# Recurrence levels of a chunked scan on one TensorE: 64 query columns in place of 128 in the products and the masked copies

## The chip, the cores and the metric

The kernel runs on one core of one Trainium2 chip. The metric is the device time of one execution in microseconds (us); the time before is the median of three runs. TensorE is called PE, VectorE DVE, ScalarE ACT, GpSimd POOL and SyncE SP, as in the profile.

## What is computed

The reference is a two-layer hybrid block (convolution, attention, a gated recurrence, a Fourier mix) followed by a second block (latent attention, a state-space model, a feed-forward network), on 1024 positions and 256 positions of context, all in float32. The change lies in the gated recurrence of the first block. Its reference, cut to the core:

```python
def step(state, inp):
    qc, kc, vc, lf = inp
    a = jnp.cumsum(lf, axis=2)
    a_last = a[:, :, -1:, :]
    s_new = jnp.exp(a_last)[:, :, 0, :, None] * state + jnp.einsum(
        "bhsk,bhsv->bhkv", kc * jnp.exp(a_last - a), vc)
    ...
    inter = jnp.einsum("bhtk,bhkv->bhtv", qc * jnp.exp(a), state)
    diff = a[:, :, :, None, :] - a[:, :, None, :, :]
    dec = jnp.exp(jnp.where(causal, diff, -jnp.inf))
    scores = jnp.einsum("bhtk,bhsk,bhtsk->bhts", qc, kc, dec)
    intra = jnp.einsum("bhts,bhsv->bhtv", scores, vc)
    return s_new, inter + intra
```

There are four heads of 64 channels, two directions and two layers, so `recurrence` runs four times.

## The kernel before

**Levels.** The kernel works on chunks of 128 positions. The decay between key s and query t inside a chunk can't be split into a factor of s and a factor of t for all pairs at once, so the pairs are sorted into seven levels, `LEVELS = [64, 32, 16, 8, 4, 2, 1]` (h), and an eighth step for s = t. At level h the chunk falls into blocks of 2h positions; in the forward direction the first half of each block holds keys and the second half queries (`query_half` is 1; in the backward direction it is 0). The tile `x` (`X[j % 2][:, l, c, :]`, 128 positions for each level l and each pair of heads c) holds the scaled keys in the one half and the scaled queries in the other. The function `halves` gives views of both.

**One chunk on each engine** (u counts chunks, j those with an output):
- POOL (L1167, L1168) writes differences of `a` into `x`, 14 operations of 128 elements per chunk, for a chunk two further on, when the products that read this buffer are done.
- ACT exponentiates `eq` (L1180), `ke` (L1184, twice) and all of `x` (L1190, 1792 elements), and copies the turned keys `ket` out of PSUM (L1196).
- PE does, in this order: the products of levels 0 and 1 (L1327), two transposes of `ke` (L1303), the products of levels 2 to 5 (L1327), in layer 0 a piece of another matrix product (the modulation, `mods.products`, L2640 and L2643, weights read from memory), the products of level 6 and of the diagonal (`q,key`), the state products (L1337), and last the eight output products (L1347 and L1348), which need the finished `sc`. One product is four matmuls, one for each head: stationary operand `x` (64 rows, 128 columns), moving operand also `x`. The heads of a pair lie on partitions 0 to 63 and 64 to 127 and write different PSUM banks. A float32 matmul shows as two records.
- DVE gathers the scores: eight `copy_predicated` (L1259) per chunk, which take from PSUM into `sc` those elements that the level's mask selects. Between them it scales the level operands of the next chunk: after the second copy `ke` and `qe` (L1220, L1225), from the third copy on two `tensor_tensor` of 128 elements (L1238) per level. Then come the state update (L1271) and the copy or addition of the output into `o` (L1281, L1283).

**What sets the order.** Everything is written by hand. The eight steps are done in pairs g (two levels, one PSUM region for each parity of g). A copy waits for `products` of its pair; the first matmul of a pair waits until the copies of the pair two before are done (`masked`, two copies per pair): so the last pair (level 6 and diagonal) waits for the copy of level 3. The output products wait for all eight copies. I call the eight copies c0 to c7.

Layer 0 has ten chunks with output per direction and the modulation product in each, layer 1 has eight and no modulation product (its two context chunks give a state only).

Of the kernel before, what the change touches and what calls it, by code (L numbers as in the profile page):

```python
# [9 lines left out]
U32 = mybir.dt.uint32  # L10
F32R = mybir.dt.float32r

P = 128
# [7 lines left out]
HD = 64  # L21
# [986 lines left out]
LEVELS = [64, 32, 16, 8, 4, 2, 1]  # L1008
NL = len(LEVELS)
# [102 lines left out]
def recurrence(k, direction, q, key, a, v, o, outputs, lay, mods=None):  # L1112
# [7 lines left out]
    nc, ps, d = k.nc, k.ps, k.d  # L1120
# [5 lines left out]
    sc = lay("sc", [P, 2, 2, P])  # L1126
# [15 lines left out]
    def halves(view, h):  # L1142

        r = view.rearrange("p c (n s h) -> p c n s h", s=2, h=h)
        return [r[:, :, :, i, :] for i in range(2)]

    with nc.Block() as block:
# [53 lines left out]
        @block.vector  # L1201
        def _(dve):
            n = [0]

            def link(ins):

                ins.then_inc(chain, 1)
                n[0] += 1
                dve.wait_ge(chain, n[0])

            dve.memset(sc[:, :, :, :], 0.0)
            link(dve.memset(S[0][:, :, :], 0.0))
            dve.wait_ge(masks_in, 16)

            def scale(u):

                t = order[u]
                qs, ks = q[:, :, t * P:(t + 1) * P], key[:, :, t * P:(t + 1) * P]
                dve.wait_ge(exped, u + 1)
                dve.tensor_tensor(ke[:, :, :], ke[:, :, :], ks, ALU.mult).then_inc(scaled, 1)  # L1220
                if want[u]:
                    j = n_out[u]
                    if j >= 2:
                        dve.wait_ge(o_ready, j - 1)
                    dve.tensor_tensor(qe[j % 2][:, :, :], eq[u % 2][:, :, :], qs, ALU.mult).then_inc(scaled, 1)  # L1225

            def scale_level(u, l):

                if u >= len(order) or not want[u]:
                    return  # L1230
                t, j, h = order[u], n_out[u], LEVELS[l]
                qs, ks = q[:, :, t * P:(t + 1) * P], key[:, :, t * P:(t + 1) * P]
                if l == 0:
                    dve.wait_ge(x_exped, j + 1)
                xh = halves(X[j % 2][:, l, :, :], h)
                f = [halves(ks, h)[0], halves(qs, h)[1]] if query_half else [halves(qs, h)[0], halves(ks, h)[1]]
                for i in range(2):
                    ins = dve.tensor_tensor(xh[i], xh[i], f[i], ALU.mult)  # L1238
                if l == NL - 1:
                    ins.then_inc(scaled, 1)  # L1240

            def finish(u):

                t = order[u]
                if not want[u] and u + 1 < len(order):
                    scale(u + 1)
                    for l in range(NL):
                        scale_level(u + 1, l)
                if want[u]:
                    j = n_out[u]  # L1250
                    if j >= 1:
                        dve.wait_ge(o_ready, j)
                    for l in range(NL + 1):
                        g, half = PAIRS * j + l // 2, l % 2
                        dve.wait_ge(products, g + 1)
                        if l:
                            dve.wait_ge(masked, (NL + 1) * j + l)
                        b = 2 * (g % 2)
                        dve.copy_predicated(  # L1259
                            sc[:, :, :, :].rearrange("p a b c -> p (a b) c"),  # L1260
                            masks[:, l, :].bitcast(U32).unsqueeze(1).to_broadcast([P, 4, P]),
                            ps[:, b:b + 2, half * 256:half * 256 + 256].rearrange("p a (b c) -> p a b c", b=2)
                        ).then_inc(masked, 1)
                        if l == 1 and u + 1 < len(order):
                            scale(u + 1)
                        if l >= 2:
                            scale_level(u + 1, l - 2)
                    scale_level(u + 1, NL - 1)
                dve.wait_ge(s_ready, u + 1)
                for c in range(2):  # L1270
                    ins = dve.scalar_tensor_tensor(S[(u + 1) % 2][:, c, :], S[u % 2][:, c, :],  # L1271
                                                   eq[u % 2][:, c, edge:edge + 1],
                                                   ps[:, 4, BR + c * HD:BR + (c + 1) * HD], ALU.mult, ALU.add)
                ins.then_inc(state_out, 1)
                if want[u]:
                    j = n_out[u]
                    dve.wait_ge(o_ready, j + 1)
                    src = ps[:, 6:8, 0:P].rearrange("p a (c e) -> p a c e", c=2)
                    dst = o[:, t, :].rearrange("p (c a e) -> p a c e", c=2, a=2)
                    if direction == 0:  # L1280
                        dve.tensor_copy(dst, src).then_inc(o_out, 1)  # L1281
                    else:
                        dve.tensor_tensor(dst, src, dst, ALU.add).then_inc(o_out, 1)  # L1283
                dve.wait_ge(state_out, u + 1)

            scale(0)
            for l in range(NL):
                scale_level(0, l)
            for u in range(len(order)):
                finish(u)  # L1290

        @block.tensor
        def _(pe):
            scales = 0
            for u, t in enumerate(order):
                j = n_out[u]

                def turn_keys():
                    pe.wait_ge(scaled, base + 1)
                    if u >= 1:  # L1300
                        pe.wait_ge(state_out, u)
                    for c in range(2):
                        mm = pe.transpose(ps[:, 4, c * P:(c + 1) * P], ke[:, c, :], k.ident[:, :])  # L1303
                    mm.then_inc(ke_t, 1)

                base = scales
                scales += 1
                if not want[u]:
                    turn_keys()
                else:  # L1310
                    scales += 2
                    pe.wait_ge(scaled, scales)
                    for l in range(NL + 1):
                        g, half = PAIRS * j + l // 2, l % 2
                        if g >= 2 and half == 0:
                            pe.wait_ge(masked, 2 * (g - 1))
                        for h in range(4):
                            c, par = divmod(h, 2)
                            p0 = par * HD
                            if l < NL:  # L1320
                                x = X[j % 2][p0:p0 + HD, l, c, :]
                                y = x
                            else:
                                x = key[p0:p0 + HD, c, t * P:(t + 1) * P]
                                y = q[p0:p0 + HD, c, t * P:(t + 1) * P]
                            o0 = half * 256 + c * P
                            mm = pe.matmul(ps[:, 2 * (g % 2) + par, o0:o0 + P], x, y, start=True, stop=True)  # L1327
                        if half:
                            mm.then_inc(products, 1)
                        if l == 1:  # L1330
                            turn_keys()
                        if l == 5 and mods:
                            mods.products(pe, mods.first + u)
                pe.wait_ge(ket_out, u + 1)
                for h in range(4):
                    c, p0 = h // 2, (h % 2) * HD
                    mm = pe.matmul(ps[p0:p0 + HD, 4, BR + c * HD:BR + (c + 1) * HD], ket[:, h * HD:(h + 1) * HD],  # L1337
                                   v[:, t, h * HD:(h + 1) * HD], start=True, stop=True)
                mm.then_inc(s_ready, 1)
                if want[u]:  # L1340
                    if j >= 1:
                        pe.wait_ge(o_out, j)
                    pe.wait_ge(masked, (NL + 1) * (j + 1))
                    for h in range(4):
                        c, p0 = h // 2, (h % 2) * HD
                        out = ps[:, 6 + h % 2, c * HD:(c + 1) * HD]
                        pe.matmul(out, sc[:, h % 2, c, :], v[:, t, h * HD:(h + 1) * HD], start=True, stop=False)  # L1347
                        mm = pe.matmul(out, qe[j % 2][p0:p0 + HD, c, :], S[u % 2][p0:p0 + HD, c, :], start=False, stop=True)  # L1348
                    mm.then_inc(o_ready, 1)
# [1960 lines left out]
```

## Time and profile before

| | |
|---|---|
| Median of three runs | 5587.69 us (5578.17 to 5592.48) |
| The profiled execution | 5573.2 us, of which the span is 5571.4 us |
| PE busy | 4363.7 us (78% of the span) |
| DVE busy | 2794.4 us (50%) |
| Mean granted PE clock, whole span | 0.861 of full |
| The four recurrences together (from the first operation to the last output) | 617.1 us |

Busy time of an engine is the sum of its instructions' durations; the granted clock is the share of 2.4 GHz that PE was given, and in the rows it is either 0.5 (1.2 GHz, here "the low level") or 1.0 (2.4 GHz, "the high level"). Times in rows count from the start of the span.

### The profile page before, as it was taken

The numbers are of one execution on the slowest core, as the hardware profiler recorded it, in microseconds if no ns is written. First come the engines' busy times: TensorE is split into PE (matmuls) and PEld (weight loads), VectorE is DVE, ScalarE is ACT, GpSimd is POOL, SyncE is SP. The second block draws the span as 40 slices with busy tenths as digits, with TensorE's granted clock in tenths as the row PEclk, the third lists the DMA queues.
The fourth block names the chain that finished last, engine by engine and source line by source line (L and its number), as shares of the span: only waits on it lengthen the run. The fifth ranks groups of instructions, "written<-read, shape, count | busy, mean of one in ns | idle before, by whom it ended". The sixth has DMA issues, their size and how long they took to land. (4 is left out here: it accounts for less than half of the span.)

```text
span 5571.4 us, 56250 instructions
## 1 busy us (share of the span) xinstructions
PE 4363.7 (78%) x21480; PEld 3260.8 (59%) x21480; DVE 2794.4 (50%) x3679; ACT 1861.5 (33%) x3198; POOL 1655.8 (30%) x1452
## 2 busy tenths in 40 slices
PE   5758868678776984747876999998673868899898
PEld 4644557566664563536663565656552656688676
DVE  2354446564535545565543445452446755466556
ACT  3321342323432244232341333332331434344333
POOL 1321132324432132222331121212223635233355
PEclk7968887769987996757988999999886979899999
DMA  4000013223400000000400000002100044211133
GB/s 145 16 19 0 8 60 120 85 74 111 147 16 19 1 16 19 8 4 24 145 30 29 4 7 4 4 1 91 46 1 2 1 170 153 63 46 46 65 129 124
DMA packets 173533, 285.88 MB, mean 51 GB/s; under 512 B 43402, under 2 KB 98698, under 8 KB 173268
## 3 DMA queue, kind: packets, MB, share of 16 engines
q1 hardware_dynamic: 172516, 282.07, 15.0%
q8 instruction: 173, 2.83, 0.2%
q0 software_dynamic: 608, 0.08, 0.1%
q14 instruction: 92, 0.75, 0.0%
q10 hardware_dynamic: 144, 0.15, 0.0%
HBM read 257.01 MB, written 25.26 MB: 51 GB/s over the span
## 5 line engine op out<-in xcount | busy, mean ns | idle before, releaser
L303 POOL TENSOR_TENSOR w_low<-w,w_high 128x512 fp32r<-128x512 f32 (+2 forms) x336 | 505.3, 1506 | 1293.6 <-ACT w_high L294 1293.3
L315 DVE TENSOR_TENSOR x_low<-buf_a,x_high 128x1280 fp32r<-128x1280 f32 (+4 forms) x336 | 369.7, 1101 | 834.1 <-ACT x_high L290 833.7
L332 PE MATMUL ps<-x_high,w_high 128*128 128x256 f32 (+1 forms) x1344 | 499.3, 372 | 93.6 <-POOL w_low L303 86.7
L290 ACT CAST x_high<-buf_a 128x1280 fp32r<-128x1280 f32 (+4 forms) x336 | 310.1, 923 | 777.8 <-PE ps L334 657.6
L945 ACT ACTIVATE pt<-ps 128x512 f32<-128x512 f32 (+1 forms) x488 | 289.6, 594 | 743.9 <-PE ps L888 742.3
L2779 POOL TENSOR_TENSOR w_low<-w,w_high 128x1024 fp32r<-128x1024 f32 x170 | 413.0, 2433 | 347.5 <-ACT w_high L3001 347.4
L898 PE MATMUL ps<-pt,v 128*128 128x512 f32 (+1 forms) x976 | 504.6, 599 | 0.0
L333 PE MATMUL ps<-x_low,w_high 128*128 128x256 f32 (+1 forms) x1344 | 491.2, 365 | 0.0
L334 PE MATMUL ps<-x_high,w_low 128*128 128x256 f32 (+1 forms) x1344 | 486.2, 362 | 0.0
L3031 PE MATMUL ps<-w_high,x_high 128*128 128x512 f32 x896 | 369.3, 412 | 130.3 <-POOL w_low L2779 92.7
L969 DVE TENSOR_REDUCE mx<-ps 128x1 f32<-128x1280 f32 (+1 forms) x200 | 289.7, 1449 | 341.6 <-PE ps L855 340.2
L332 PEld LDWEIGHTS ps<-x_high,w_high 128*128 128x128 f32 x1344 | 263.0, 196 | 172.9 <-issue 70.6
L3032 PE MATMUL ps<-w_low,x_high 128*128 128x512 f32 x896 | 361.0, 403 | 0.0
L3033 PE MATMUL ps<-w_high,x_low 128*128 128x512 f32 x896 | 360.2, 402 | 0.0
L1327 PE MATMUL ps<-x 64*128 64x128 f32 x2016 | 223.0, 374 | 103.0 <-DVE x L1238 87.2
L3001 ACT CAST w_high<-w 128x1024 fp32r<-128x1024 f32 x170 | 178.4, 1049 | 369.8 <-PE ps L3033 369.6
L886 PE MATMUL ps<-q_high,k_high 97*128 97x512 f32 (+3 forms) x488 | 289.7, 594 | 11.1 <-DVE q_low L982 11.1
L332 PE MATMUL ps<-w_high,x_high 128*128 128x512 f32 (+2 forms) x608 | 218.4, 359 | 99.2 <-POOL w_low L303 98.7
L991 DVE RECIPROCAL rec<-ps 64x512 f32<-64x512 f32 (+1 forms) x52 | 168.1, 3232 | 249.5 <-PE ps L898 249.5
L2335 PE MATMUL ps<-x_high,w_high 128*128 128x512 f32 x704 | 278.6, 396 | 13.2 <-DVE x_low L2430 13.2
L3031 PEld LDWEIGHTS ps<-w_high,x_high 128*128 128x128 f32 x896 | 175.5, 196 | 191.3 <-issue 152.8
L334 PEld LDWEIGHTS ps<-x_high,w_low 128*128 128x128 f32 x1344 | 261.7, 195 | 40.5
(388 smaller groups left out, 9354.7 us busy)
## 6 DMA issues: line engine op xcount, KB each, us to landing
w<-in_w_out SPq DMA_DIRECT2D x26, 2048.0 KB, 7.9
w<-in_w_mod SPq DMA_DIRECT2D x24, 2048.0 KB, 8.1
w<-in_w_down SPq DMA_DIRECT2D x15, 2048.0 KB, 7.8
w<-in_w_in SPq DMA_DIRECT2D x12, 2048.0 KB, 10.8
w<-in_w_up SPq DMA_DIRECT2D x22, 1024.0 KB, 6.5
w<-in_w_in SPq DMA_DIRECT2D x16, 1024.0 KB, 5.0
x<-in_x SPq DMA_DIRECT2D x16, 512.0 KB, 3.5
scratch_x<-x SPq DMA_DIRECT2D x16, 512.0 KB, 5.3
```

Source lines behind the costliest of these rows:

```text
L290: act.copy(xh[i % NX][:, 0:s["tn"]], x_of(s)).then_inc(x_high, 1)
L303: pool.tensor_tensor(wl[i % NW][:, 0:n], w_of(s), wh[i % NW][:, 0:n].bitcast(F32), ALU.subtract).then_inc(w_low, 1)
L315: dve.tensor_tensor(xl[i % NX][:, 0:s["tn"]], x_of(s), xh[i % NX][:, 0:s["tn"]].bitcast(F32), ALU.subtract).then_inc(x_low, 1)
L332: pe.matmul(g["out"], lhs[0][:, :], rhs[0][:, :], start=(s["kk"] == 0), stop=False)
L333: pe.matmul(g["out"], lhs[0][:, :], rhs[1][:, :], start=False, stop=False)
L334: mm = pe.matmul(g["out"], lhs[1][:, :], rhs[0][:, :], start=False, stop=s["last"])
L886: pe.matmul(o, hi, qh[u % 2][r0:r1, 0:nq], start=True, stop=False)
L898: pe.matmul(ps[:, 6 + u % 2, 0:w["nq"]], w["v"](i), pt[g % NPT][:, 0:w["nq"]], start=(i == 0), stop=(i == n - 1)).then_inc(pv_done, 1)
L2779: pool.tensor_tensor(wl[i % NW][:, :], ws.tile(s["chunk"])[:, s["kk"] % PER, :], wh[i % NW][:, :].bitcast(F32), ALU.subtract).then_inc(w_l ...
L3031: pe.matmul(o, a[:, t], wh[i % NW][:, c], start=(s["kk"] == 0), stop=False)
L3032: pe.matmul(o, a[:, t], wl[i % NW][:, c], start=False, stop=False)
L3033: mm = pe.matmul(o, b[:, t], wh[i % NW][:, c], start=False, stop=s["last"])
```

## The change

Of the 128 columns of a level's scores the mask selects only those at query positions, which are 64. The change makes the moving operand of each level product the query half alone (64 columns, contiguous for h = 64, and in runs of h with a step of 2h otherwise), puts the two levels of a pair side by side in 256 columns of PSUM for each pair of heads, and copies under the mask only the 64 query columns of each head, into the same places of `sc`. The diagonal step keeps 128 columns in both. The stationary operand stays all 128 columns of `x`. The number and order of instructions and all waits stay.

```diff
-                        dve.copy_predicated(
-                            sc[:, :, :, :].rearrange("p a b c -> p (a b) c"),
-                            masks[:, l, :].bitcast(U32).unsqueeze(1).to_broadcast([P, 4, P]),
-                            ps[:, b:b + 2, half * 256:half * 256 + 256].rearrange("p a (b c) -> p a b c", b=2)
-                        ).then_inc(masked, 1)
+                        heads = ps[:, b:b + 2, :].rearrange("p a (c x) -> p (a c) x", c=2)
+                        if l < NL:
+                            h = LEVELS[l]
+                            n_blocks = P // (2 * h)
+                            to = sc[:, :, :, :].rearrange("p a c (n s h) -> p (a c) n s h", s=2, h=h)[:, :, :, query_half, :]
+                            which = masks[:, l, :].rearrange("p (n s h) -> p n s h", s=2, h=h)[:, :, query_half, :]
+                            dve.copy_predicated(
+                                to, which.bitcast(U32).unsqueeze(1).to_broadcast([P, 4, n_blocks, h]),
+                                heads[:, :, half * HD:half * HD + HD].rearrange("p g (n h) -> p g n h", h=h)
+                            ).then_inc(masked, 1)
+                        else:
+                            dve.copy_predicated(
+                                sc[:, :, :, :].rearrange("p a c t -> p (a c) t"),
+                                masks[:, l, :].bitcast(U32).unsqueeze(1).to_broadcast([P, 4, P]),
+                                heads[:, :, half * HD:half * HD + P]).then_inc(masked, 1)
...
                                 x = X[j % 2][p0:p0 + HD, l, c, :]
-                                y = x
+                                y = halves(X[j % 2][p0:p0 + HD, l, :, :], LEVELS[l])[query_half][:, c]
...
-                            o0 = half * 256 + c * P
-                            mm = pe.matmul(ps[:, 2 * (g % 2) + par, o0:o0 + P], x, y, start=True, stop=True)
+                            o0, m = c * 256 + half * HD, HD if l < NL else P
+                            mm = pe.matmul(ps[:, 2 * (g % 2) + par, o0:o0 + m], x, y, start=True, stop=True)
```

The first chunk of the first recurrence on PE, as the program issues it before the change. A row gives the line, the output and inputs, the output's partitions x columns, and how many follow each other:

```order
L1327 MATMUL ps<-x_140_5781 128x128 x8
L1303 MATMUL ps<-ident_49,ke_5787 128x128 x2
L1327 MATMUL ps<-x_140_5781 128x128 x16
L2640 MATMUL ps<-w_2_50,act_c_55 2x128 x32
L2643 MATMUL ps<-bias_135_5777,one_56 2x128 x4
L1327 MATMUL ps<-x_140_5781 128x128 x4
L1327 MATMUL ps<-q_4404,key_4406 128x128 x4
```

The same place after the change (line numbers are ten higher):

```order
L1337 MATMUL ps<-x_140_5781 128x64 x8
L1313 MATMUL ps<-ident_49,ke_5787 128x128 x2
L1337 MATMUL ps<-x_140_5781 128x64 x16
L2650 MATMUL ps<-w_2_50,act_c_55 2x128 x32
L2653 MATMUL ps<-bias_135_5777,one_56 2x128 x4
L1337 MATMUL ps<-x_140_5781 128x64 x4
L1337 MATMUL ps<-q_4404,key_4406 128x128 x4
```

Nothing has moved; the 28 level matmuls of a chunk stream 64 columns where they streamed 128.

On DVE, the same chunk from the copy of level 0 on, before the change (the last number is what one instruction writes per partition):

```order
L1259 COPY_PREDICATED sc_5789<-masks_5790,ps 128x512 x2
L1220 TENSOR_TENSOR ke_5787<-ke_5787,key_4406 128x256
L1225 TENSOR_TENSOR qe_145_5786<-eq_143_5784,q_4404 128x256
L1259 COPY_PREDICATED sc_5789<-masks_5790,ps 128x512
L1238 TENSOR_TENSOR x_141_5782<-x_141_5782,key_4406 128x2x64
L1238 TENSOR_TENSOR x_141_5782<-x_141_5782,q_4404 128x2x64
L1259 COPY_PREDICATED sc_5789<-masks_5790,ps 128x512
```

And after it:

```order
L1265 COPY_PREDICATED sc_5789<-masks_5790,ps 128x4x64
L1265 COPY_PREDICATED sc_5789<-masks_5790,ps 128x8x32
L1220 TENSOR_TENSOR ke_5787<-ke_5787,key_4406 128x256
L1225 TENSOR_TENSOR qe_145_5786<-eq_143_5784,q_4404 128x256
L1265 COPY_PREDICATED sc_5789<-masks_5790,ps 128x16x16
L1238 TENSOR_TENSOR x_141_5782<-x_141_5782,key_4406 128x2x64
L1238 TENSOR_TENSOR x_141_5782<-x_141_5782,q_4404 128x2x64
L1265 COPY_PREDICATED sc_5789<-masks_5790,ps 128x32x8
```

Here too only sizes change: seven of the eight copies write 256 elements per partition in place of 512, in shorter runs with each level (the eighth, for the diagonal, keeps 512).

## Rows read from the trace of the kernel before

**Rows 1.** The page, part 1: busy us (share of the span) xinstructions.
```profile
PE 4363.7 (78%) x21480; PEld 3260.8 (59%) x21480; DVE 2794.4 (50%) x3679; ACT 1861.5 (33%) x3198; POOL 1655.8 (30%) x1452
```

**Rows 2.** Windows (length, PE, PEld, DVE, ACT, POOL busy, clock, DMA), layers 0, 1.
```profile
811.00:981.00 170.00, 137.14 (x1620) 115.20 (x1620) 107.78 (x272) 40.31 (x91) 55.66 (x140) 0.70 0.36 122
2184.00:2321.70 137.70, 94.86 (x740) 79.74 (x740) 87.34 (x224) 26.65 (x49) 44.45 (x112) 0.70 0.02 5
```

**Rows 3.** Timeline, one layer 0 chunk: start us, us, engine, line [idle before <-releaser].
```profile
901.60 2.12 PE L1327 MATMUL ps<-x 64*128 64x128 f32 x15
...
903.85 1.56 DVE L1259 COPY_PREDICATED sc<-masks,ps 128x512 f32<-128x512 uint32 x2 [1.49 <-PE ps L1327]
904.26 2.44 PE L1327 MATMUL ps<-x 64*128 64x128 f32 x32
905.67 0.43 DVE L1220 TENSOR_TENSOR ke<-ke,key 128x256 f32<-128x256 f32 x1 [0.26 <-ACT ke L1184]
906.64 1.93 PE L2640 MATMUL ps<-w,act_c 128*2 128x128 f32 x64
907.26 0.29 DVE L1238 TENSOR_TENSOR x<-x,key 128x128 f32<-128x128 f32 x1 [0.17 <-ACT x L1190]
908.50 0.40 PE L2643 MATMUL ps<-bias,one 1*2 1x128 f32 x8
909.37 0.61 PE L1327 MATMUL ps<-q,key 64*128 64x128 f32 x8
910.95 0.71 DVE L1259 COPY_PREDICATED sc<-masks,ps 128x512 f32<-128x512 uint32 x1
```

**Rows 4.** Timeline, c6 of the chunk before that one.
```profile
895.35 0.73 DVE L1259 COPY_PREDICATED sc<-masks,ps 128x512 f32<-128x512 uint32 x1 [0.16 <-PE ps L1327]
```

**Rows 5.** Timeline, one layer 1 chunk, copies c0, c3, c6, c7 and the outputs.
```profile
2462.36 1.56 DVE L1259 COPY_PREDICATED sc<-masks,ps 128x512 f32<-128x512 uint32 x2 [1.49 <-PE ps L1327]
...
2466.18 0.72 DVE L1259 COPY_PREDICATED sc<-masks,ps 128x512 f32<-128x512 uint32 x1
...
2469.45 0.72 DVE L1259 COPY_PREDICATED sc<-masks,ps 128x512 f32<-128x512 uint32 x1
2470.66 0.71 DVE L1259 COPY_PREDICATED sc<-masks,ps 128x512 f32<-128x512 uint32 x1
2471.52 0.41 PE L1347 MATMUL ps<-v,sc 128*128 128x64 f32 x2 [3.02 <-DVE sc L1259]
2476.28 0.42 DVE L1283 TENSOR_TENSOR o<-ps,o 128x256 f32<-128x256 f32 x1 [3.07 <-PE ps L1348]
```

**Rows 6.** Timeline, the output copies that bound the periods.
```profile
839.33 0.42 DVE L1281 COPY o<-ps 128x256 f32<-128x256 f32 x1 [3.25 <-PE ps L1348]
965.10 0.42 DVE L1281 COPY o<-ps 128x256 f32<-128x256 f32 x1 [4.00 <-PE ps L1348]
2214.06 0.42 DVE L1281 COPY o<-ps 128x256 f32<-128x256 f32 x1 [3.27 <-PE ps L1348]
2307.33 0.42 DVE L1281 COPY o<-ps 128x256 f32<-128x256 f32 x1 [3.04 <-PE ps L1348]
2492.37 0.42 DVE L1283 TENSOR_TENSOR o<-ps,o 128x256 f32<-128x256 f32 x1 [3.33 <-PE ps L1348]
```

**Rows 7.** Windows around the chunk of rows 3.
```profile
898.30:905.10 6.80, 6.80 (x38) 5.66 (x40) 2.43 (x7) 0.73 (x3) 2.57 (x7) 0.50 0.48 184
905.10:911.90 6.80, 5.27 (x124) 4.37 (x122) 6.37 (x18) 3.15 (x7) 1.82 (x5) 1.00 0.28 66
```

**Rows 8.** Line L1942: matmuls of 16 columns on 128-column weights; one window of it.
```profile
L1942 PE MATMUL ps<-dta,tri x40: 374/374/392, 4238.5 to 4246.8; 128*128 128x16 f32 x40
...
4239.00:4246.00 7.00, 7.00 (x35) 7.00 (x34) 0.00 (x0) 0.00 (x0) 0.00 (x0) 0.50 0.00 0
```

**Rows 9.** Timeline, eight records of 64 columns and what follows them.
```profile
4318.06 1.00 PE L2128 MATMUL ps<-xd,e 128*128 128x64 f32 x8
4318.87 0.48 PE L2113 MATMUL ps<-sums_at_t,sums_at_s 128*128 128x512 f32 x1
```

## The prediction

> **What bounds the kernel now.** Over the whole span PE is the busiest engine at 78% [rows 1], but this says little about four stages of 617 us together. So I read the windows of the recurrences first: one in layer 0 takes 170 us with PE busy 137 and DVE 108, one in layer 1 137.7 us with 94.9 and 87.3, and the mean granted clock is 0.70, below the 0.861 of the kernel [rows 2]. Neither engine is full: it is a ring of waits, once round per chunk. The ring's period comes from the output copies: (965.10 - 839.33)/8 = 15.72 us in layer 0 and (2307.33 - 2214.06)/6 = 15.55 us in layer 1 [rows 6].
>
> Next the timeline of a chunk, following in the brackets what ended each idle time. In layer 1 [rows 5]: c0 starts at 2462.36; the reader should see that c3 starts 3.82 later, c7 8.30 later, and the output products 9.16 later, released by DVE. From there PE runs the eight output products and the next chunk's first two levels, and only then can the next c0 start: at the low clock level the period is 2492.37 - 2476.28 = 16.09, so this second half takes 16.09 - 9.16 = 6.93. The ring is thus DVE (c0 to c7), PE (outputs, levels 0 and 1), DVE. Two waits inside the DVE half are for ACT, not for a copy: `ke` at 905.67 (idle 0.26) and the first scaling at 907.26 (idle 0.17, until the big exponential is done) [rows 3]. So what c0, c1 and c2 take is hidden behind ACT; from 907.26, just before c3, DVE runs on its own. In layer 0 a third wait can come in: PE has the modulation product (64 records) ahead of level 6 and the diagonal. Those end at 909.37 + 0.61 = 909.98, 0.97 before c6 in this chunk [rows 3], but in the chunk before it c6 waited for PE [rows 4]. There PE and DVE are level.
>
> **The change, part by part.**
>
> *Copies, 512 to 256 elements.* No 256-element masked copy is in the trace. The nearest: a `tensor_tensor` of 256 elements takes 0.43 and one of 128 takes 0.29 [rows 3], 1.1 ns per element; 256 fewer elements save 0.27 or 0.28 of 0.72. The scalings at L1238 have the same broken-up runs and the one at h = 64 is no faster than its fellows, so I charge nothing for the short runs. c0 to c2 lie behind ACT: nothing. c3 to c6 are on the path: 4 x 0.27 = 1.07 us per chunk at most, c7 is unchanged. Bounds: 0 if runs cost what is saved, 1.1.
>
> *Level products, 128 to 64 moving columns.* Here the stationary operand decides. 35 records of 16 columns on weights of 128 columns fill a window of 7.00 us at the low level, 0.20 each [rows 8]. The level products of 128 columns use the two row halves side by side, so their records come in pairs: 15 records in 2.12 us at the low level, with the tail of the last one in it (a record lasts 0.37 in a slot of 0.20 in rows 8): 0.25 per pair or a little less [rows 3]. At the high level eight records of 64 columns take 4318.87 - 4318.06 = 0.81, 0.10 each [rows 9], and 16 pairs of 128 columns, the first of them still at the low level, 906.64 - 904.26 = 2.38, 0.15 per pair [rows 3]. So an eighth of the columns does not bring a record below 0.20; half of them brings nothing. The sum takes 0 per record; bound: half of it, 0.1 per pair at the low level, 0.8 for levels 0 and 1. The Trainium skill, TensorE: Matmul & The Clock Gate, section "Back-to-back issue gap", gives the spacing of an isolated matmul as proportional to its moving columns; by it these products would take half, which is rival 3, and the trace with its 0.20 for 16 columns does not bear it out where each record loads new weights.
>
> *The clock.* This is the term I weigh most. Now the low level lasts through the output products and levels 0 and 1, PE busy all of 6.80 us, and turns high at 905.1, when 128-column products have run since before 901.60 [rows 3, 7]. In rows 8 PE is just as busy, 7.00 of 7.00 us, yet the level stays low to the end: the records there stream 16 columns and spend the rest on weights. So a PE busy with loading weights does not raise the level; one that streams does. After the change each level record streams half of what its slot holds, as the output products do, under which the level doesn't rise either. I take it that in layer 1 the level now stays low all through, and in layer 0 it rises only under the modulation product, whose moving side is unchanged.
>
> The same page of the Trainium skill, in its part on the HAM clock gate, says that how busy PE has recently been decides the clock. Read as the profile's busy share it would leave the level as it is, which is rival 1; rows 8 (busy 7.00 of 7.00, clock 0.50) speak against that reading.
>
> **Layer 1 with the low level throughout.** Levels 2 to 5 are 16 pairs at 0.2, from 904.26 - 903.85 = 0.41 after c0 [rows 3] to 0.41 + 3.3 = 3.7: before c4, no wait. Level 6 and the diagonal start when c3 ends, 3.82 + 0.45 = 4.3, take eight pairs of records at 0.2 and 0.25 for signals, 1.9, and end at 6.2. c6 would come at (2469.45 - 2462.36) - 3 x 0.27 = 6.3 [rows 5]: just hidden. Outputs start at 9.16 - 1.07 = 8.1, then 6.93: period 15.0 against 15.55. Over 2 x 8 chunks -0.55 x 16 = **-9 us**.
>
> **Layer 0.** PE after c0: 0.41 + 3.3, modulation 908.50 - 906.64 = 1.86 at the high level [rows 3], 3.7 at the low one, bias 0.3 or 0.6, level 6 and the diagonal 909.98 - 908.50 - 0.3 = 1.2 or 1.9. All low: 9.9; high from the start of the modulation: 7.1. c6 then waits for PE (it would be ready at 6.3); behind it come c6 and a scaling, 1.21 - 0.27 = 0.94, c7 to outputs 2471.52 - 2470.66 = 0.86 [rows 5], and 0.15 of signal: 1.95. Period all low 9.9 + 1.95 + 6.93 = 18.8; high from the modulation on 7.1 + 1.95 + 6.93 = 16.0, against 15.72. The level needs the streaming work first, so I take the middle of these two, 17.4: +1.7 x 20 = **+34 us**. Bounds +0.3 x 20 = +6 and +3.1 x 20 = +62.
>
> **Sum.** +34 - 9 = +25 us. The profiled execution took 5573.2, with 1.8 outside the span, which gives 5598; the median of runs lies 14.5 above it, so 5587.7 + 25, rounded to **5612 us**. 0.3% is 17 us, and this is about what a measurement of this kernel can tell from no change. The likeliest case's own range is -5 to +55 us: 5583 to 5643.
>
> **Rivals.**
> 1. *The level behaves as now; only the shorter copies count. Faster.* Layer 1: -1.07 x 16 = -17. Layer 0: c6 gains up to 0.97 where PE was early [rows 3] and about 0.3 (its own length) where it waited [rows 4]: -0.65 x 20 = -13; and PE's idle time before the outputs shrinks from 3.02 [rows 5] to about 2, so that more output products may still find the high level, each chunk where they do gaining up to half of 4.8 us. Together -30 to -50, say -38: 5550 us. For it: PE's busy share hardly changes. Against it: rows 8. It decides if the clock rows still show 1.0 in layer 1. Chance 0.22.
> 2. *The level falls in layer 1 but in layer 0 rises early in the modulation product: a draw.* Between 16.0 and 16.5 in layer 0, +6 to +16, less 9: within 0.3%, about 5590 us. For it: the modulation streams at full rate. Against: before it lie 3.3 us of half-empty products. Chance 0.20.
> 3. *Moving columns set the pace after all.* Levels 0 and 1 save 0.8 at the low level, the rest of PE's part shrinks as well, slots are full of streaming and the level rises as now: -(0.8 + 1.07) x 36 = -67 us, 5521. Rows 8 speak against. Chance 0.05.
> 4. *The copies don't get shorter* (runs of 1 and 2 elements with a step, 128x128x2): layer 1 gives +0.5 x 16 = +8 in place of -9, the whole +45 or more: 5633. L1238 speaks against. Chance 0.03.
>
> **Numbers.** My forecast has 0.50. Slower by over 0.3%: the forecast and rival 4, 0.53. Within: rival 2, 0.20. Faster: rivals 1 and 3, 0.27. The range reaches from 5538 (rival 1 at its far end) to 5643 (the upper end of the forecast) and leaves rival 3, and the case of low level throughout layer 0, outside.
>
> **What the profile after would show.** Copies at the new line near 0.45 us, c7 at 0.71. Clock in the window of a layer 1 recurrence near 0.50 (0.70 before), and in layer 0 about 0.60 to 0.65. In layer 1 idle before c6 close to zero, period 15.0; in layer 0 idle time before c6 of 1 to 3 us, released by PE's level products, period 17 to 17.5. Modulation records spread over more than 1.93 us in most chunks. What would prove me wrong: a clock of 1.0 inside a layer 1 recurrence; 16-record groups of levels 0 and 1 in about half of 2.4 us; or layer 0 chunks of 16 us or less.

## The result, and the profile of the changed kernel

The changed kernel takes 5615.6 us (median of six runs, 5604.6 to 5617.0), the kernel before 5583.6 (six runs, 5573.5 to 5593.9). The ratio is 1.0053, with the 95% interval 1.0038 to 1.0069: slower, by 32 us between the medians.

Page, part 1, of the changed kernel, as [rows 1] for before:

```profile
PE 4446.0 (79%) x21480; PEld 3318.7 (59%) x21480; DVE 2740.6 (49%) x3679; ACT 1861.4 (33%) x3198; POOL 1651.0 (29%) x1452
```

DVE is busy 54 us less, as meant. PE streams fewer columns in 2016 of its records and is busy 82 us more. Windows (length, busy times of PE, PEld, DVE, ACT, POOL, then clock, DMA) over both recurrences of layer 0 and of layer 1, first of the kernel before, then of the changed one:

```profile
811.00:1213.00 402.00, 305.27 (x3384) 255.13 (x3384) 242.34 (x582) 109.97 (x213) 127.09 (x288) 0.71 0.30 102
2184.00:2553.00 369.00, 221.61 (x1624) 185.29 (x1624) 216.96 (x504) 97.42 (x143) 103.09 (x232) 0.68 0.02 6
```

```profile
811.00:1242.00 431.00, 340.18 (x3384) 274.52 (x3384) 214.64 (x582) 109.95 (x213) 123.71 (x288) 0.64 0.28 95
2218.00:2585.00 367.00, 254.09 (x1624) 216.42 (x1624) 191.80 (x504) 97.52 (x143) 101.58 (x232) 0.54 0.02 7
...
2230.00:2310.00 80.00, 69.47 (x465) 60.26 (x465) 47.85 (x146) 14.27 (x25) 27.38 (x70) 0.50 0.00 1
```

The same 3384 and 1624 records take PE 35 and 32 us longer, at a clock of 0.64 and 0.54 where it was 0.71 and 0.68; in the window inside a layer 1 recurrence (third row of the changed kernel) it is 0.50. Layer 0 grew by 29 us, layer 1 shrank by 2. Timeline of one layer 1 chunk, c0 to the next c0, to be read against [rows 5]:

```profile
2264.61 0.98 DVE L1265 COPY_PREDICATED sc<-masks,ps 128x256 f32<-128x256 uint32 x2 [1.38 <-PE ps L1337]
...
2268.02 0.29 DVE L1238 TENSOR_TENSOR x<-x,key 128x128 f32<-128x128 f32 x1 [0.48 <-ACT x L1190]
...
2268.43 0.42 DVE L1265 COPY_PREDICATED sc<-masks,ps 128x256 f32<-128x256 uint32 x1
...
2269.16 0.42 DVE L1265 COPY_PREDICATED sc<-masks,ps 128x256 f32<-128x256 uint32 x1
...
2269.82 1.17 PE L1337 MATMUL ps<-q,key 64*128 64x128 f32 x8
2269.90 0.72 DVE L1265 COPY_PREDICATED sc<-masks,ps 128x256 f32<-128x256 uint32 x1
...
2271.03 0.72 DVE L1265 COPY_PREDICATED sc<-masks,ps 128x256 f32<-128x256 uint32 x1
2271.07 0.40 POOL L1167 TENSOR_TENSOR x<-a 128x128 f32<-128x128 f32 x1 [9.89 <-PE ps L1337]
...
2271.90 0.48 DVE L1238 TENSOR_TENSOR x<-x,q 128x128 f32<-128x128 f32 x1
...
2272.31 0.71 DVE L1270 COPY_PREDICATED sc<-masks,ps 128x512 f32<-128x512 uint32 x1
...
2273.17 0.66 PE L1357 MATMUL ps<-v,sc 128*128 128x64 f32 x2 [1.56 <-DVE sc L1270]
...
2277.73 2.12 PE L1337 MATMUL ps<-x 64*128 64x64 f32 x15
...
2279.98 0.44 DVE L1265 COPY_PREDICATED sc<-masks,ps 128x256 f32<-128x256 uint32 x1 [1.38 <-PE ps L1337]
```

Four things are to be seen. The fifteen records of 64 columns take 2.12 us, to the digit what fifteen of 128 took [rows 3]. The copies c0 to c4 take 0.42 to 0.45 us, but c5 (h = 2, at 2269.90) and c6 (h = 1, at 2271.03) take 0.72, as the copies of 512 elements did. Before the scaling ahead of c3 stands the same wait for ACT as before the change, only that it is now 0.48 long in place of 0.17 [rows 3]: this is where the shorter c0 to c2 went, and c3 starts 3.82 after c0 as before [rows 5]. And when POOL starts (2271.07), DVE's scaling behind it takes 0.48 in place of 0.29. The ring: outputs 2273.17 - 2264.61 = 8.56 after c0 (9.16 before), next c0 6.81 after that (before: 6.93 where the output products ran at the low level, but 5.95 to 6.95 from chunk to chunk of layer 1, as some ran at the high level). c3 to c7 takes 3.88, before the change 4.48: 0.60 saved of the 1.07 forecast.

Timeline of one layer 0 chunk:

```profile
895.15 0.98 DVE L1265 COPY_PREDICATED sc<-masks,ps 128x256 f32<-128x256 uint32 x2 [1.38 <-PE ps L1337]
895.57 3.68 PE L1337 MATMUL ps<-x 64*128 64x64 f32 x32
...
899.17 3.23 PE L2650 MATMUL ps<-w,act_c 128*2 128x128 f32 x64
...
903.15 0.66 PE L1337 MATMUL ps<-q,key 64*128 64x128 f32 x8
...
903.86 0.73 DVE L1265 COPY_PREDICATED sc<-masks,ps 128x256 f32<-128x256 uint32 x1 [2.39 <-PE ps L1337]
...
906.00 0.66 PE L1357 MATMUL ps<-v,sc 128*128 128x64 f32 x2 [1.80 <-DVE sc L1270]
...
912.82 0.98 DVE L1265 COPY_PREDICATED sc<-masks,ps 128x256 f32<-128x256 uint32 x2 [1.38 <-PE ps L1337]
```

The 32 records of levels 2 to 5 take 3.68 us where they took 2.44, the 64 of the modulation 3.23 where they took 1.93 [rows 3]. By the windows of this chunk the granted clock is 0.50 up to 901 and 1.00 from 902 to 904, so the level rises 2 to 3 us into the modulation product, and by 906 it is 0.50 again; before the change it rose at 905.1, ahead of that product [rows 3, 7]. Of the recurrence's products only the last run at the high level (eight of the diagonal in 0.66, in layer 1 1.17). So c6 (at 903.86) waits 2.39 us for PE, and this chunk lasts 912.82 - 895.15 = 17.67 us. Output copies of the first recurrences of layer 0 and layer 1, with the first and the last but one of each:

```profile
841.45 0.42 DVE L1291 COPY o<-ps 128x256 f32<-128x256 f32 x1 [3.03 <-PE ps L1358]
...
911.02 0.42 DVE L1291 COPY o<-ps 128x256 f32<-128x256 f32 x1 [3.35 <-PE ps L1358]
926.67 0.42 DVE L1291 COPY o<-ps 128x256 f32<-128x256 f32 x1 [1.62 <-PE ps L1358]
944.71 0.43 DVE L1291 COPY o<-ps 128x256 f32<-128x256 f32 x1 [3.34 <-PE ps L1358]
...
978.08 0.43 DVE L1291 COPY o<-ps 128x256 f32<-128x256 f32 x1 [3.76 <-PE ps L1358]
2247.43 0.42 DVE L1291 COPY o<-ps 128x256 f32<-128x256 f32 x1 [3.28 <-PE ps L1358]
...
2339.35 0.43 DVE L1291 COPY o<-ps 128x256 f32<-128x256 f32 x1 [4.00 <-PE ps L1358]
```

Periods, over the same eight and six chunks as in [rows 6]: (978.08 - 841.45)/8 = 17.08 us in layer 0 (short ones of 15.65 and long ones of 18.04 stand next to each other) and (2339.35 - 2247.43)/6 = 15.32 in layer 1, against 15.72 and 15.55. The last period of a recurrence is shorter than the others, and it is not among them: in layer 1 it was 13.34 before (2307.33 to 2320.67) and is 14.47 now (2339.35 to 2353.82).

### The profile page after: what moved, and what is told of

Same layout as the page of the kernel before. It is cut to its first block and busy times, and to the rows that moved or that the text cites. A ratio compares the mean times of both kernels' runs of the same rounds, so it can differ in the third digit from the quotient of the medians.

```text
span 5615.2 us, 56250 instructions
## 1 busy us (share of the span) xinstructions
PE 4446.0 (79%) x21480; PEld 3318.7 (59%) x21480; DVE 2740.6 (49%) x3679; ACT 1861.4 (33%) x3198; POOL 1651.0 (29%) x1452
## 5 line engine op out<-in xcount | busy, mean ns | idle before, releaser
L1337 PE MATMUL ps<-x 64*128 64x64 f32 x2016 | 247.4, 410 | 90.0 <-DVE x L1238 87.2
L1337 PEld LDWEIGHTS ps<-x 64*128 64x128 f32 x2016 | 228.5, 316 | 110.9 <-DVE x L1238 88.4
```

The source lines that it names most:

```text
L1337: mm = pe.matmul(ps[:, 2 * (g % 2) + par, o0:o0 + m], x, y, start=True, stop=True)
```

## The experiments

All kernels are variants of the changed one. The ratio is to the kernel before, run on the same chip (its median there was 5580.6 for e1 to e4, 5583.4 for e5 to e7, 5582.6 for e8 to e10), with its 95% interval. The last three columns come from each profile: from the first operation of the first recurrence of a layer to the start of the last output copy of its second, so 20 chunks with output in layer 0 and 16 in layer 1.

| kernel | median us | ratio (interval) | layer 0 us | layer 1 us | sum |
|---|---|---|---|---|---|
| before | 5583.6 | 1 | 401.4 | 368.0 | 769.4 |
| changed | 5615.6 | 1.0053 (1.0038 to 1.0069) | 430.3 | 366.0 | 796.3 |
| e1 stream 128, copy 64 | 5567.0 | 0.9974 (0.9964 to 0.9984) | 395.6 | 355.9 | 751.5 |
| e2 stream 64, copy 128 | 5617.9 | 1.0064 (1.0048 to 1.0080) | 429.1 | 369.3 | 798.4 |
| e3 e1, c0 to c2 full | 5565.2 | 0.9968 (0.9957 to 0.9979) | 396.7 | 357.7 | 754.4 |
| e4 mask packed | 5610.7 | 1.0050 (1.0037 to 1.0063) | 430.3 | 366.1 | 796.4 |
| e5 e1, h = 1 first | 5563.6 | 0.9968 (0.9955 to 0.9980) | 393.9 | 352.9 | 746.8 |
| e6 h = 1 writes packed | 5608.0 | 1.0046 (1.0031 to 1.0061) | 429.7 | 360.2 | 789.9 |
| e7 stream 128 in layer 0 only | 5571.7 | 0.9980 (0.9972 to 0.9989) | 395.3 | 365.5 | 760.8 |
| e8 e1, h = 1, 2 first | 5544.7 | 0.9932 (0.9918 to 0.9946) | 384.1 | 348.3 | 732.4 |
| e9 h = 1, 2 write packed | 5609.4 | 1.0049 (1.0034 to 1.0064) | 429.6 | 360.3 | 789.9 |
| e10 e8, POOL later | 5524.6 | 0.9897 (0.9881 to 0.9913) | 378.1 | 334.9 | 713.0 |

The sum of the stages moves with the medians (e10 - before: -56.4 against 5524.6 - 5582.6 = -58.0), within about 5 us but for e9 (6) and e2 (8). The rest of the span is the same work in all of them and (between the layers and behind them) takes between 3990 and 4008 us from profile to profile. In the five kernels with 64 streamed columns in both layers the median has risen 3 to 8 us more than the stages; where this part lies isn't shown.

### The two halves of the change: e1 and e2

e1 streams all 128 columns again (the two halves of each block sorted, so that the query columns lie side by side) and keeps the copies of 256 elements:

```diff
-y = halves(X[j % 2][p0:p0 + HD, l, :, :], LEVELS[l])[query_half][:, c]
+y = X[j % 2][p0:p0 + HD, l, c, :].rearrange("p (n s h) -> p s n h", s=2, h=LEVELS[l])
...
-o0, m = c * 256 + half * HD, HD if l < NL else P
+o0, m = c * 256 + half * P, P
...
-    heads[:, :, half * HD:half * HD + HD].rearrange("p g (n h) -> p g n h", h=h)
+    heads[:, :, half * P + query_half * HD:half * P + query_half * HD + HD].rearrange("p g (n h) -> p g n h", h=h)
```

> The level products stream all 128 columns again (the same 64 query columns plus the 64 key columns, in the order half, block, position, so that the query columns lie together in PSUM); the copies take 64 columns as in the changed kernel. Only the streamed columns differ from the changed kernel. Theory (the columns that PE streams set the clock level, and the level is what the change lost): the high level comes back in layer 1, mean clock of a recurrence near 0.70 as before the change, layer 1 period about 14.6 to 15.0, layer 0 about 15.0; time 25 to 45 us under the kernel before, about 5550. Rival (the level fell because the shorter copies or the new place in PSUM changed the rhythm, not because of the columns): clock stays 0.50 in layer 1 and the time stays at 5600 or more.

e2 is the other half alone: 64 columns streamed, every copy 512 elements (it takes 128 columns from where 64 hold the level's scores, so its output is not the reference's).

```diff
-                        if l < NL:
+                        if False:
...
-heads[:, :, half * HD:half * HD + P]
+heads[:, :, (half * HD if l == NL else 0):(half * HD if l == NL else 0) + P]
```

> The level products stream 64 columns as in the changed kernel, the copies have 512 elements as before the change, all from columns 0 to 127 of each half bank (they put wrong scores into sc, so that the output isn't the reference's; durations are what counts). Theory: the low level throughout layer 1, period there 16.1 (before: 15.55 and 15.76), layer 0 chunks as long as in the changed kernel, about 17; time about 12 us over the changed kernel, 5627. Rival (fewer columns cost nothing, the loss lies in the copies): as the kernel before, 5584.

e1 is faster than before, by 14.5 us by the ratio, less than expected (5567 in place of 5550). e2 is slower by 36: all of the loss, and not distinguishable from the changed kernel, as the intervals overlap. It was expected 12 us above the changed kernel and came out 2 above; the last timeline of the experiments shows why. Windows of e1 in layer 0 and layer 1:

```profile
830.00:960.00 130.00, 114.12 (x1411) 95.68 (x1409) 78.38 (x235) 33.14 (x77) 43.84 (x112) 0.73 0.37 126
2230.00:2310.00 80.00, 61.33 (x499) 52.13 (x497) 48.67 (x143) 13.19 (x22) 22.28 (x56) 0.72 0.00 1
```

In the same 80 us of layer 1 PE carries 499 records in 61.33 us at 0.72; the changed kernel carried 465 in 69.47 at 0.50. Between e1 and the changed kernel the instructions, their order, the waits and the sizes of the copies are the same; the streamed columns differ, and with them where the products lie in PSUM. The place was not tested by itself, but the kernel before and e1 stream 128 columns into different places and show the same clock (0.68 over layer 1 in both), and e2 has the low level with the full copies. So it is the streamed columns that the level follows here, and streaming 64 in place of 128 costs 796.3 - 751.5 = 44.8 us of the stages.

### Which layer: e7

e7 streams 128 columns in layer 0 (where `mods` is set) and 64 in layer 1:

```diff
+if mods:
+    y = X[j % 2][p0:p0 + HD, l, c, :].rearrange("p (n s h) -> p s n h", s=2, h=LEVELS[l])
+else:
     y = halves(X[j % 2][p0:p0 + HD, l, :, :], LEVELS[l])[query_half][:, c]
```

> 128 columns streamed in layer 0 alone, 64 in layer 1, 64 copied in both. Theory (the loss of the changed kernel lies in layer 0, where the modulation product and level 6 behind it run at the low level): layer 0 chunks as in the first experiment (15.4), layer 1 as in the changed kernel (clock 0.50, period 15.37); time about 5 us over the first experiment, 5572, ratio 0.998. Rival (the low level in layer 1 costs as much per chunk as in layer 0): half of the loss stays, 5590.

It came out at 5571.7, as expected. The windows show each layer at its own level:

```profile
830.00:960.00 130.00, 114.09 (x1333) 95.58 (x1332) 76.66 (x230) 31.95 (x76) 43.86 (x112) 0.72 0.39 134
2230.00:2310.00 80.00, 71.53 (x482) 62.08 (x482) 46.26 (x139) 14.64 (x26) 21.89 (x56) 0.50 0.00 1
```

The low level costs 430.3 - 395.3 = 35.0 us in layer 0, where PE ends last before c6, and only 365.5 - 355.9 = 9.6 in layer 1, where DVE does: there the outputs start 8.56 us after c0 at the low level and 8.47 in e1, and what is lost lies behind them (6.82 to the next c0, in e1 5.5 to 7.0).

### Are c0 to c2 hidden: e3

e3 is e1 with c0, c1 and c2 copying 512 elements again.

```diff
+if l < 3:
+    dve.copy_predicated(
+        sc[:, :, :, :].rearrange("p a c t -> p (a c) t"),
+        masks[:, l, :].bitcast(U32).unsqueeze(1).to_broadcast([P, 4, P]),
+        heads[:, :, half * P:half * P + P]).then_inc(masked, 1)
+elif l < NL:
```

> As the first experiment, but the copies of levels 0, 1 and 2 have 512 elements again (the output is the same). Theory: these three lie behind ACT's exponentials, so the time is that of the first experiment within 3 us. Rival: every shorter copy counts; then 3 x 0.27 x 36 = 29 us are lost against the first experiment.

0.9968 against 0.9974, intervals that lie on each other, where the rival had 29 us (0.5%): what three of the eight copies take costs nothing that can be measured, as the wait for ACT before c3 said.

### Why c5 and c6 stay at 0.72 us: e4, e5, e6, e9

The copy of level h writes runs of h elements with a step of 2h, and reads its mask likewise; the PSUM side is contiguous. e4 puts the mask of h = 1 side by side in a free half of another level's mask:

```diff
+if h == 1:
+    which = masks[:, 0, free:free + HD].rearrange("p (n h) -> p n h", h=1)
```

> The changed kernel with the mask of the last level (h = 1) packed once per recurrence into 64 contiguous columns, so that its copy reads the mask without a step; the destination keeps its step of two elements. In the changed kernel this copy takes 0.72 us and the six others of 256 elements 0.42 to 0.44. If the step of the mask is the cause: 0.44, and 0.28 x 36 = 10 us less than the changed kernel, 5605. If the step of the destination is the cause: 0.72 still, and no change of the time.

e6 leaves the mask and writes the scores of h = 1 side by side (to places where they don't belong, so its output is not the reference's); e9 does so for h = 1 and h = 2:

```diff
+if h == 1:
+    to = sc[:, :, :, 0:HD].rearrange("p a c (n h) -> p (a c) n h", h=1)
```

> The changed kernel, but the copy of h = 1 writes columns 0 to 63 of each head without a step (the wrong places, so that the output isn't the reference's); its mask keeps the step. If the destination's step of two elements makes this copy slow: 0.44 us in place of 0.72, and about 9 us less than the changed kernel, 5606. If it is the step of the mask and the destination only together, or the run length of one element as such: 0.72 and no change.

> The changed kernel, with the copies of h = 2 and h = 1 both writing columns 0 to 63 of each head without a step (the wrong places, so that the output isn't the reference's). If a destination in runs of 1 or 2 elements is what makes them slow, both take 0.44 us: copy after copy 0.74 apart up to c5 and no 0.72 left but that of the diagonal. Time: 0.28 less than with h = 1 packed alone in layer 1 unless level 6's products (ending 6.37 after c0) come later than c6 could start (6.03): then no further gain, 5608.

e5 is e1 with another order of the levels, `LEVELS = [1, 64, 32, 16, 8, 4, 2]`, so that the copy of h = 1 is c0 and lies behind ACT:

> The first experiment (128 columns streamed, 64 copied) with the levels in the order 1, 64, 32, 16, 8, 4, 2, so that the copy of h = 1 (0.72 us for 256 elements) is c0, which lies behind ACT, and c6 is h = 2 (0.44). Theory (only c3 to c6 are on the path): c6 takes 0.43, period 0.2 to 0.3 us shorter in layer 1 and in the layer 0 chunks too, since c6 stands behind every wait there: 0.28 x 34 = about 9 us less than the first experiment, ratio to the kernel before about 0.996. Rival (the order is indifferent): as the first experiment, 0.9974.

The copies c5 and c6 in one layer 1 chunk, first of e4, then of e6:

```profile
2268.35 0.72 DVE L1269 COPY_PREDICATED sc<-masks,ps 128x256 f32<-128x256 uint32 x1
2269.48 0.73 DVE L1269 COPY_PREDICATED sc<-masks,ps 128x256 f32<-128x256 uint32 x1
```

```profile
2268.59 0.72 DVE L1267 COPY_PREDICATED sc<-masks,ps 128x256 f32<-128x256 uint32 x1
...
2269.72 0.45 DVE L1267 COPY_PREDICATED sc<-masks,ps 128x256 f32<-128x256 uint32 x1
2269.76 0.40 POOL L1167 TENSOR_TENSOR x<-a 128x128 f32<-128x128 f32 x1 [9.54 <-PE ps L1339]
```

With the mask packed c6 still takes 0.73; with the destination packed it takes 0.45. All copies of e9, by the view of the tile `sc`, and those of the changed kernel (min/median/max ns):

```profile
L1267 DVE COPY_PREDICATED sc<-masks,ps x252: 418/440/450, 825.3 to 2572.1; 128x256 f32<-128x256 uint32 x126
```

```profile
L1265 DVE COPY_PREDICATED sc<-masks,ps x252: 418/441/734, 825.1 to 2577.5; 128x256 f32<-128x256 uint32 x126
```

So the step of the destination is the cause, for runs of one and of two elements; with both packed nothing is above 0.45. My first theory put the blame on h = 1 alone, though c5, the copy of h = 2, stands at 0.72 in the trace of the changed kernel; e5, in which c6 is the copy of h = 2 and still takes 0.72, refuted it. So e5 did not bring the 9 us expected of it: it lies 3 us below e1 by the ratios, within the intervals, and 4.7 by the stages. For the time it matters little as long as the level is low: e6 and e9 save 6 us of stages, all in layer 1, and e9 no more than e6, since c6 then waits for PE's products (0.31 us in the chunk whose c0 is at 2264.12). e4, e6 and e9 kept the loss (+26 to +28 us by the ratios): the cause of the +32 isn't there.

### What the copies are worth when PE doesn't hold them up: e8 and e10

e8 is e1 with `LEVELS = [1, 2, 64, 32, 16, 8, 4]`: both slow copies are now c0 and c1.

> 128 columns streamed, 64 copied, levels in the order 1, 2, 64, 32, 16, 8, 4. In the traces so far the copies of h = 1 and of h = 2 take 0.72 us, those of h = 4 and above 0.42 to 0.44. Here the two slow ones are c0 and c1, which lie behind ACT, and c3 to c6 all take 0.42 to 0.44. Theory: up to 0.28 us per chunk less than with h = 1 alone in front, but GpSimd's operations run beside the scalings from c5 on and may take part of it: 4 to 9 us less, about 5557, ratio 0.995 to 0.996. Rival (behind c5 GpSimd sets DVE's pace, whatever the copies take): no change from 0.9968.

It is 22 us faster than e1 by the medians and 19 faster than e5, where 4 to 9 were expected. Of the 14.4 us of stages between e5 and e8, 9.8 lie in layer 0, where the period went from 15.36 to 14.93; why so much, I haven't settled. In layer 1 the outputs start 8.46 us after c0 (within 0.02) in e1, e5 and e8 alike, though c5 and c6 became shorter: something still stood between the copies. Timeline of e8, c5 to the outputs:

```profile
2223.36 0.43 DVE L1265 COPY_PREDICATED sc<-masks,ps 128x256 f32<-128x256 uint32 x1
2223.63 0.40 POOL L1167 TENSOR_TENSOR x<-a 128x128 f32<-128x128 f32 x1 [9.81 <-PE ps L1337]
2223.69 0.49 DVE L1238 TENSOR_TENSOR x<-x,key 128x128 f32<-128x128 f32 x1
...
2224.10 0.48 DVE L1238 TENSOR_TENSOR x<-x,q 128x128 f32<-128x128 f32 x1
...
2224.51 0.42 DVE L1265 COPY_PREDICATED sc<-masks,ps 128x256 f32<-128x256 uint32 x1
...
2226.53 0.41 PE L1357 MATMUL ps<-v,sc 128*128 128x64 f32 x2 [2.61 <-DVE sc L1270]
```

The step from c5 to c6 is 1.15 us, from c4 to c5 it was 0.73 (0.43 and two scalings of 0.29, each overlapping the next): as soon as the products are done POOL begins on the chunk two further on, and each scaling takes 0.48. e10 lets POOL wait for the copies:

```diff
-                    pool.wait_ge(products, PAIRS * (j - 1))
+                    pool.wait_ge(masked, (NL + 1) * (j - 1))
```

> As the kernel with h = 1 and h = 2 in front, but POOL starts its subtractions when the eight copies of a chunk are done, not when its products are. Theory: the scalings between c5, c6, c7 and the outputs, which take 0.48 while POOL runs and 0.28 when it doesn't, are short again, POOL works while DVE waits for the output products, and the outputs start 0.5 to 0.8 us earlier: 15 to 25 us less than without it. Rival (POOL then comes too late for ACT's exponential): the first scaling of a chunk waits longer than 3.4 us after c0 and the time rises.

```profile
2213.04 0.42 DVE L1265 COPY_PREDICATED sc<-masks,ps 128x256 f32<-128x256 uint32 x1
...
2213.77 0.42 DVE L1265 COPY_PREDICATED sc<-masks,ps 128x256 f32<-128x256 uint32 x1
...
2214.50 0.72 DVE L1270 COPY_PREDICATED sc<-masks,ps 128x512 f32<-128x512 uint32 x1
...
2215.30 0.96 POOL L1167 TENSOR_TENSOR x<-a 128x128 f32<-128x128 f32 x1 [7.32 <-DVE sc L1270]
...
2215.37 0.41 PE L1357 MATMUL ps<-v,sc 128*128 128x64 f32 x2 [1.77 <-DVE sc L1270]
```

c5 to c6 is 0.73, c5 to the outputs 2.33 in place of 3.17. The outputs now start 7.62 us after c0. e10 takes 5524.6 us, 20 less than e8, as expected, and 1.0% less than the kernel before: the best version found. It holds one half of the change only, the copies of 64 columns, and none of the saving on PE; the order of the levels and POOL's later start are outside the change, and neither was tried on the kernel before by itself.

The same contention, seen from its other side, shows in e2. Timeline of one layer 1 chunk of e2, whose copies all have 512 elements:

```profile
2263.30 1.56 DVE L1270 COPY_PREDICATED sc<-masks,ps 128x512 f32<-128x512 uint32 x2 [1.38 <-PE ps L1337]
...
2270.75 0.27 DVE L1238 TENSOR_TENSOR x<-x,key 128x128 f32<-128x128 f32 x1
2270.80 0.69 POOL L1167 TENSOR_TENSOR x<-a 128x128 f32<-128x128 f32 x1
...
2271.81 1.09 POOL L1167 TENSOR_TENSOR x<-a 128x128 f32<-128x128 f32 x1
...
2272.01 0.66 PE L1357 MATMUL ps<-v,sc 128*128 128x64 f32 x2 [1.43 <-DVE sc L1270]
```

Here the products end later, POOL starts later after c0 (6.75; before 5.84, changed 6.46), and the two engines meet the other way round: DVE's scalings keep their 0.28 and POOL's operations take 0.69 and 1.09 in place of 0.40. The outputs start 8.71 after c0, where the kernel before with the same copies needed 9.16; in its chunk without POOL (c0 at 2294.56) they started 8.72 after c0. So POOL cost the kernel before 0.44 us in most layer 1 chunks, and e2's period there is 15.53, not 16.1.

## Why the prediction was right, and where its terms were off

The time was forecast at 5612 and measured at 5615.6; the forecast case, the low level in layer 1 and a late rise in layer 0, is the one that came. By its steps:

- **"Half of them brings nothing" (moving columns): right.** 2.12 us for fifteen records before and after; rival 3 falls.
- **The clock: right, and shown.** 0.50 in layer 1, as forecast, and 0.64 in layer 0 (0.60 to 0.65). e1, e2 and e7 separate it from the copies: streaming 64 costs 44.8 us of stages, 35.0 in layer 0. Rival 1, by which the level stays and only the copies count, did not come, but e1 is that case built on purpose: it gives 5567, where I had 5550.
- **Layer 0: +34 forecast, +29 measured** (401.4 to 430.3). The period went to 17.08 in place of 17.4. I had taken the middle between 16.0 and 18.8 and called it a middle; the chunks do lie on both sides, 15.65 and 18.04 next to each other. What decides from chunk to chunk where in the modulation product the level rises, I haven't settled. A mean period of 18.8, the low level throughout, did not come; the prediction calls it outside its range, but by its own terms +62 - 9 = +53 us lies just inside the +55.
- **Layer 1: -9 forecast, -2 measured.** The period is 15.32 over six chunks and 15.37 in the chunk shown, forecast 15.0. The last period, which the forecast took for one like the others, grew by 1.1 us in the first recurrence and 1.3 in the second. The outputs start 8.56 after c0 where I had 8.1. The second half was 6.81 against 6.93. The kernel before had this 6.93 only where its outputs ran at the low level. c6 was forecast "just hidden", products ending at 6.2 and c6 at 6.3; they end at 2269.82 + 1.17 - 2264.61 = 6.38 and c6 starts at 6.42.
- **The copies: the mis-sized term.** The step that failed is "I charge nothing for the short runs", with its "4 x 0.27 = 1.07 us per chunk at most". c3 and c4 saved 0.3 each, c5 and c6 nothing: 0.60 in all. The rows of L1238 from which I argued have equally short runs in what they write and take 0.27 to 0.29 us at every level where POOL is idle, and are no guide: it is another instruction. e6 and e9 show that the same copies take 0.45 when they write side by side. In layer 0 it made no difference, since c6 waited for PE there (2.39 in the chunk shown).
- **c0 to c2 "hidden behind ACT: nothing": right** (e3).
- **A term that was missing: POOL beside DVE.** The scalings were costed at one duration. They can be longer while POOL runs, and POOL starts when the products end. In the chunks shown the forecast got away with it: two scalings before c7 were long before the change and two after it. But it is 0.45 us per chunk where they meet POOL otherwise (e2), and 19 us of stages once PE and the copies are out of the way (e8 to e10). In e1 too scalings before c7 are long; that this is part of why e1 brought 14.5 us and not the 25 to 45 expected is argued, not shown by a run of its own.

The two errors in layer 0 (+34 for +29) and layer 1 (-9 for -2) cancel to 2 us; that the total of the stages, +25 against +26.9, agrees so well is partly luck. The measured +32 has some 5 us more than the stages show, within what the rest of the span varies, and that the median came within 4 us of the forecast is luck too.

The parts don't add up on their own. Shorter copies are worth 769.4 - 751.5 = 17.9 us with 128 streamed columns (before to e1) and 798.4 - 796.3 = 2.1 with 64 (e2 to changed). Seen the other way, streaming 64 costs 798.4 - 769.4 = 29.0 us with the full copies (27.7 of it in layer 0, 1.3 in layer 1) and 44.8 with the short ones. In layer 0 (429.1 to 430.3) the saving on DVE is lost because PE ends last before c6. In layer 1 (369.3 to 366.0) DVE had no such wait in e2; there the outputs move only from 8.71 to 8.56 after c0, because in the changed kernel c6 comes when the products end and the scalings behind it are lengthened by POOL, as they are not in e2.

## What to carry to other kernels

Streaming 64 columns in place of 128 saved nothing here, where each matmul loads its own 128 columns of weights, and it cost the clock: look at the granted clock of such stretches before and after, and if it falls, try keeping the columns. Take the two halves of such a change apart; the half that trims DVE was a gain of its own. On DVE, put masked copies that write runs of one and two elements where they are hidden, and where the traces show GpSimd and DVE lengthening each other, try having GpSimd's work wait until the chain of DVE is done.

## What was not expected of the hardware

- A `copy_predicated` of 256 float32 elements per partition takes 0.42 to 0.45 us when the destination has runs of 4 or more elements, and 0.72 to 0.73 when the runs are 1 or 2 long (step 2 or 4). The step in the mask is not the cause: without it the copy still takes 0.73 (e4), and with it, but written side by side, 0.45 (e6, e9). The Trainium skill, SBUF — State Buffer, in its note on SBUF cachelines (section "Door 1: The DMA port swizzle"), says that float32 may be strided over up to four elements for free; for this instruction's destination the measurement says otherwise.
- A `tensor_tensor` of 128 elements on DVE takes 0.28 us alone and up to 0.48 or 0.5 while GpSimd's `tensor_tensor` runs (e8, changed); or it keeps its 0.28 and GpSimd's takes 0.69 to 1.09 in place of 0.40 (e2, e10). The Trainium skill, SBUF — State Buffer, section "Who interferes with whom", says that a DVE instruction with two SBUF inputs contends with a GpSimd instruction that reads SBUF; the trace agrees, 0.48 against 0.28, and the other way round GpSimd's first operation in e10 takes 0.96 in place of 0.40 beside scalings of 0.29. What decides which of the two gives way was not tested.
- PE stays at the low level with a busy share of 87% (69.47 of 80 us in layer 1, clock 0.50), while e1, with the same instructions and twice the streamed columns, shows 0.72 with a share of 77% (61.33 of 80 us): here the higher busy share in the profile went with the lower clock.
